# The 32 rows of u beside the gates: 8 matmuls of 512 columns and 8 of 256 in place of 24 of 256, and the sum of the two halves on ScalarE and VectorE

## The chip, the core and the metric

The kernel runs on one core of a Trainium2 chip. The metric is the device time of one execution in microseconds (us); the number of a kernel is the median over its runs.

## The reference

One launch computes two transformer blocks over 256 tokens of width 1024, in float32. The last part of the second block, an expert layer (PEER), is what the change touches. It has 128 x 128 experts; every token and each of 8 heads picks 16 of them, with a softmax weight (the gate) each.

```python
# x: (256, 1024) normed tokens; u, v: (16384, 1024), one row per expert
G[t, e] = sum over heads and picks of the softmax weight of token t for expert e
hid     = gelu_tanh(x @ u.T) * G          # (256, 16384)
h       = h + hid @ v
out     = rmsnorm(h) * final_norm_g_2
```

The kernel computes hid densely: 128 rows of u, each of 128 experts (128 x 1024 weights, 512 KB), and 128 rows of v of the same size.

## The kernel before

**Number format.** A product in full float32 precision is made of three products of rounded numbers (fp32r): w_hi * x_hi, w_hi * x_lo and w_lo * x_hi, all summed in PSUM. x_hi and x_lo stand beside each other in the tile `x_both`. ScalarE makes w_hi out of the raw weights (L426, two halves of 512 columns for a unit), another engine makes w_lo = raw - w_hi (L433). There are two buffers of w_hi and w_lo, so the split of a unit waits for the matmuls of the unit two before it, half by half (semaphores s_use1 for the first half, s_use for the second).

**Stages of the expert layer.** 36 rows of u are multiplied early, while the picks are made. Then comes the stage of the gates, in which this change lies: it makes the matrix G, 64 groups of 4 tokens, and multiplies 32 more rows of u beside it. In this text the rows of the stage are numbered r = 0 to 31, and groups A(r) = 2r and B(r) = 2r + 1 belong to row r. The gelu of each of these 68 rows goes to memory (`early_rows`) and comes back later. After this follow the stage of v (68 rows of v, L2985 before the change, `v_unit`), and a last stage with the remaining 60 rows of both.

**One row of the stage of the gates**, each engine in its own fixed order, written out by hand:
- VectorE (DVE), `hot_body`: for a group, one instruction that makes two one-hot matrices in bf16 (L2903, from an iota in SBUF and indices in PSUM), and three that multiply one of them by three pieces of the softmax weight (L2909). There are two buffers, so group n waits until the matmuls of group n - 2 are done (s_made).
- TensorE (PE), `made_body`: 12 bf16 matmuls of 128 columns for each group (L2920), when its one-hots are there (s_hot, s_gated). Then `u_products` for each half of the row: 8 matmuls with w_hi, 256 columns each, x_hi and x_lo in turn (L509), and 4 with w_lo (L515), all into the same 256 columns of `ps_chunk[r % 2]`.
- ScalarE (ACT): copies the two groups' 4 x 128 results out of PSUM (L2927, `kept_body`), splits w_hi for row r + 2 (L426, `ahead`), takes the gelu of row r straight from PSUM (L2811, `early_gelu`), and issues the DMA to `early_rows` (L2814).
- GpSimd (POOL): w_lo for row r + 2 (L433). SyncE (SP): loads of the raw units.

The last stage already has the layout that the change brings to this one: 512 columns in one matmul with w_hi (L3102), 256 with w_lo (L3110), a copy of the second half by ScalarE (L3160), the sum by VectorE (L3214), the gelu from SBUF (L3164).

Of the kernel before, what the change touches and what calls it, by code (L numbers as in the profile page):

```python
# [20 lines left out]
ALU = mybir.AluOpType  # L21
ACT = mybir.ActivationFunctionType
AX = mybir.AxisListType

P = 128
# [190 lines left out]
def build(nc, stream, cols, rows, consts0, consts1, consts2, x, mem, positions, small_w, cmp_w1, cmp_w2, peer_keys, p_t, out):  # L216
    ctx = ExitStack()
    with ctx:
# [2603 lines left out]
        def fetch(e, q, c=0):  # L2822

            i = c * 4 + q
            src = early[i, :, :] if isinstance(i, int) else early[bass.ds(i, 1), :, :].rearrange("a p n -> p (a n)")
            e.dma_start(gel[(q + 2) % 4], src).then_inc(s_back[q % 4], 16)
# [42 lines left out]
        def peer_gates():  # L2869
# [7 lines left out]
            s_hot, s_gated, s_made, s_kept = (sem(n) for n in ("s_hot", "s_gated", "s_made", "s_kept"))  # L2877
            groups = T // 4

            def loop(e, body):  # L2880

                for g in range(4):
                    body(e, g, g)
                with e.Fori(1, groups // 4) as i:
                    for g in range(4):
                        body(e, i * 4 + g, g)

            def after(e, s, n, back):

                if not isinstance(n, int) or n >= back:  # L2890
# [39 lines left out]
            def eight_rows(c, group, row):  # L2930
                for q in range(2 * UNITS):
                    for g in (2 * q, 2 * q + 1):
                        group(c * 16 + g, g % 4)
                    for part in range(2):
                        row(c, q, part)

            def tensor_gates(e):
                def row(c, q, part):
                    i = c * 8 + (EARLY_SELECT + q)
                    if part == 0:  # L2940
                        bank_left(e, i)
                    u_products(e, q % 2, q % 2, c * 8 + (u_early + EARLY_SELECT + q), range(4 * part, 4 * part + 4), part)
                group = lambda n, g: made_body(e, n, g)
                eight_rows(0, group, row)
                with e.Fori(1, EARLY_GATES // 8) as c:
                    eight_rows(c, group, row)

            def activation_gates(e):
                def row(c, q, part):
                    if part == 0:  # L2950
                        ahead(e, q % 4, c * 2 + (EARLY_SELECT // 4 + q // 4))
                    else:
                        early_gelu(e, q, c * 8 + (EARLY_SELECT + q))
                group = lambda n, g: kept_body(e, n, g)
                for i in range(2):
                    fetch(e, i)
                eight_rows(0, group, row)
                with e.Fori(1, EARLY_GATES // 8) as c:
                    eight_rows(c, group, row)

            dve.steps.append(lambda e: loop(e, hot_body))
            pe.steps.append(tensor_gates)
            act.steps.append(activation_gates)
            for lane in work:
# [459 lines left out]
```

## Time and profile before

| | |
|---|---|
| time, median of 3 runs | 1566.6 us (1566.23 to 1568.51) |
| the profiled execution: time / span | 1562.93 us / 1561.1 us |
| mean granted clock of TensorE | 0.989 of full speed |
| busy share of the span: PE, DVE, ACT, POOL | 97%, 76%, 56%, 23% |
| stage of the gates | from 898.4 us to about 1035.5 us of the span |

Read it so: the span is the time between the first and the last instruction of the profiled execution, and stage times are counted from its start. In the timeline a piece is a merged run of like instructions: its length reaches from the start of the first to the end of the last. Matmuls are pipelined, so that a matmul's own length is more than its distance to the next one; the chain of waits counts by those distances.

### The profile page before, as it was taken

How to read it: one execution, taken by the hardware profiler on the slowest of the kernel's cores; microseconds unless marked ns; L12 is line 12 of the kernel's file. 1: busy time of each engine (PE TensorE's matmuls, PEld its weight loads, DVE VectorE, ACT ScalarE, POOL GpSimd, SP SyncE). 2: the span in 40 equal slices, each digit the busy share in tenths (PEclk: the TensorE clock that was granted, in tenths of full speed). 3: DMA queues.
4: the chain of work that ended last, by engine and by line, in shares of the span. 5: the costliest groups of instructions: out<-in, count | busy, mean ns of one | idle time of the engine just before them, and what ended most of it. 6: DMA issues, size and time to landing. Idle time of an engine off the chain costs nothing.

```text
span 1561.1 us, 31498 instructions
## 1 busy us (share of the span) xinstructions
PE 1512.0 (97%) x10240; PEld 1349.4 (86%) x10240; DVE 1187.5 (76%) x2368; ACT 870.5 (56%) x1629; POOL 355.8 (23%) x265
## 2 busy tenths in 40 slices
PE   8899998999999899899999999999999999999997
PEld 8789987999887786698999999988888888888886
DVE  4788585789748578455489978889999777777777
ACT  5664444666548654566555566654444555555555
POOL 3334333011100331232068956630000000000000
PEclk9999999999999999999999999999999999999999
DMA  8333244555665720264557755467777666666665
GB/s 291 121 109 108 92 152 148 161 183 175 197 185 173 251 81 1 68 202 149 176 162 220 231 165 156 159 187 240 241 243 239 207 193 191 189 188 188 189 190 171
DMA packets 89289, 272.22 MB, mean 174 GB/s; under 512 B 9984, under 2 KB 27520, under 8 KB 88832
## 3 DMA queue, kind: packets, MB, share of 16 engines
q1 hardware_dynamic: 65520, 238.06, 48.7%
q10 hardware_dynamic: 23696, 33.17, 6.7%
q8 instruction: 48, 0.79, 0.2%
q14 instruction: 25, 0.20, 0.0%
HBM read 259.13 MB, written 12.06 MB: 174 GB/s over the span
## 4 chain that ended last, share of the span: by engine, by line
PE 88%; DVE 6%; ACT 3%; issue 1%; DMA 1%; POOL 0%; ACTq 0%; DVEq 0%; SPq 0%
PE ps_chunk L509 17%; PE ps_misc L2985 12%; PE ps_misc L502 10%; PE ps_chunk L502 9%; PE ps_chunk L515 8%; PE ps_chunk L3102 7%; PE ps_misc L301 7%; PE ps_chunk L1947 4%; PE ps_chunk L3110 4%; PE ps_misc L2920 3%; PE ps_chunk L301 3%; PE ps_chunk L521 1%; PE ps_chunk L530 1%; PE ps_misc L1025 1%; PE ps_chunk L525 1%
## 5 line engine op out<-in xcount | busy, mean ns | idle before, releaser
L426 ACT ACTIVATE w_hi<-raw 128x512 fp32r<-128x512 f32 (+2 forms) x654 | 399.8, 625 | 364.5 <-PE ps_chunk L515 142.7
L433 DVE TENSOR_TENSOR w_lo<-raw,w_hi 128x512 fp32r<-128x512 f32 (+1 forms) x419 | 317.4, 785 | 151.5 <-ACT w_hi L426 148.4
L433 POOL TENSOR_TENSOR w_lo<-raw,w_hi 128x512 fp32r<-128x512 f32 (+2 forms) x237 | 312.4, 1328 | 499.3 <-ACT w_hi L426 432.3
L509 PE MATMUL ps_chunk<-x_both,w_hi 128*128 128x256 f32 x2208 | 314.9, 285 | 0.8 <-ACT row L2811 0.5
L509 PEld LDWEIGHTS ps_chunk<-x_both,w_hi 128*128 128x128 f32 x2208 | 284.7, 192 | 1.3 <-issue 0.7
L515 PE MATMUL ps_chunk<-x_both,w_lo 128*128 128x256 f32 x1104 | 177.4, 283 | 0.0
L515 PEld LDWEIGHTS ps_chunk<-x_both,w_lo 128*128 128x128 f32 x1104 | 152.3, 192 | 0.1
L3200 DVE TENSOR_TENSOR w_lo<-raw,w_hi 128x512 fp32r<-128x512 f32 x120 | 83.0, 693 | 67.5 <-ACT w_hi L3154 67.4
L502 PE MATMUL ps_chunk<-w_hi,x_both 128*128 128x512 f32 (+1 forms) x392 | 123.4, 396 | 5.5 <-POOL w_lo L433 2.9
L3102 PE MATMUL ps_chunk<-x_both,w_hi 128*128 128x512 f32 x480 | 120.2, 392 | 0.0
L301 PE MATMUL ps_misc<-mixers_arena 128*128 128x128 f32 (+9 forms) x820 | 110.9, 303 | 7.9 <-ACT mixers_arena L1055 3.2
L301 PEld LDWEIGHTS ps_misc<-mixers_arena 128*128 128x128 f32 (+3 forms) x820 | 94.5, 188 | 22.0 <-issue 7.9
L3154 ACT ACTIVATE w_hi<-raw 128x512 fp32r<-128x512 f32 x120 | 75.7, 632 | 63.3 <-PE ps_misc L502 63.2
L2985 PE MATMUL ps_misc<-w_hi,hid_hi 128*128 128x512 f32 x272 | 105.9, 389 | 1.0 <-issue 1.0
L2985 PE MATMUL ps_misc<-w_hi,hid_lo 128*128 128x512 f32 x272 | 105.8, 389 | 0.0
L3102 PEld LDWEIGHTS ps_chunk<-x_both,w_hi 128*128 128x128 f32 x480 | 86.4, 189 | 15.5
L502 PE MATMUL ps_misc<-w_hi,hid_hi 128*128 128x512 f32 x236 | 91.8, 389 | 0.0
L502 PE MATMUL ps_misc<-w_hi,hid_lo 128*128 128x512 f32 x236 | 91.8, 389 | 0.0
L502 PE MATMUL ps_misc<-w_lo,hid_hi 128*128 128x512 f32 x236 | 91.8, 389 | 0.0
L3026 DVE TENSOR_TENSOR xn<-row,peer_arena 128x256 f32<-128x256 f32 x128 | 82.0, 640 | 10.2 <-PE ps_misc L2985 6.9
L502 PEld LDWEIGHTS ps_chunk<-w_hi,x_both 128*128 128x128 f32 x392 | 71.5, 192 | 20.6 <-POOL w_lo L433 3.9
L502 PE MATMUL ps_chunk<-x_both,w_hi 128*128 128x256 f32 x416 | 81.3, 291 | 5.2 <-DVE w_lo L433 3.0
(437 smaller groups left out, 2635.8 us busy)
## 6 DMA issues: line engine op xcount, KB each, us to landing
raw<-in_stream SPq DMA_DIRECT2D x452, 512.0 KB, 3.8
early_rows<-row ACTq DMA_DIRECT2D x68, 128.0 KB, 2.6
row<-early_rows ACTq DMA_DIRECT2D x66, 128.0 KB, 3.4
memory_kv<-mixers_arena ACTq DMA_DIRECT2D x4, 512.0 KB, 5.0
mixers_arena<-in_cmp_w ACTq DMA_DIRECT2D x1, 2048.0 KB, 9.3
mixers_arena<-memory_kv ACTq DMA_DIRECT2D x4, 512.0 KB, 6.4
mixers_arena<-in_consts ACTq DMA_DIRECT2D x1, 1729.0 KB, 8.3
row<-in_rows ACTq DMA_DIRECT2D x3, 512.0 KB, 6.7
```

What stands on the lines that cost most here:

```text
L301: return lambda e: e.matmul(out, lhsT, rhs, start=start, stop=stop, skip_group_check=True)
L426: e.activation(w_hi[q % 2][:, s], raw[q][:, s], ACT.Copy).then_inc(made, 1)
L433: e.tensor_tensor(w_lo[q % 2][:, s], raw[q][:, s], w_hi[q % 2][:, s].bitcast(F32), ALU.subtract).then_inc(made, 1)
L502: last = e.matmul(o, stationary[a], moving[b], start=start and i == 0, stop=stop and i == 2, skip_group_check=True)
L509: e.matmul(o, w[0][:, k * P:(k + 1) * P], x[:, k, :], start=k == 0 and x is x_hi, stop=False, skip_group_check=True)
L515: last = e.matmul(o, w[1][:, k * P:(k + 1) * P], x_hi[:, k, :], start=False, stop=k == KD - 1, skip_group_check=True)
L1947: return e.matmul(out(t, half), x[:, k, t * P:(t + 1) * P], w[u % 2][:, half * CW:(half + 1) * CW], start=start, stop=stop, skip_group_che ...
L2985: return e.matmul(ps_misc[:, 2 * t + half, :], x[:, b, t * P:(t + 1) * P], weights[w][:, half * CW:(half + 1) * CW], start=start, stop=Fal ...
L3026: e.tensor_tensor(own[b], gel[slot], g, ALU.mult).then_inc(s_own, 1)
L3102: last = e.matmul(ps_chunk[b][:, 0:2 * T], w_hi[0][:, k * P:(k + 1) * P], x_both[:, :, k, :], start=k == 0, stop=False, skip_group_check=True)
L3154: e.activation(w_hi[1][:, halves[half]], raw[q][:, halves[half]], ACT.Copy).then_inc(v_high[half], 1)
L3200: e.tensor_tensor(w_lo[1][:, halves[half]], raw[q][:, halves[half]], w_hi[1][:, halves[half]].bitcast(F32), ALU.subtract).then_inc(low_mad ...
```

## The change

It does four things in the stage of the gates.
1. TensorE: with w_hi, each of the 8 blocks of 128 rows takes one matmul of 512 columns (x_hi and x_lo together, into 512 columns of `ps_chunk`) in place of two of 256. Both halves of w_hi come first, then both halves of w_lo; the s_use1 signal of the first half is thus given later within the row than before.
2. ScalarE: it copies the second 256 columns out of PSUM to SBUF (`across`, which lies in gel[2:4]), then takes the gelu in place in SBUF, when VectorE has made the sum.
3. VectorE: the sum of the two halves, `two_halves(r)`, comes behind the one-hots of groups A(r+1) and B(r+1) and ahead of those of A(r+2) and B(r+2). The wait for the DMA that empties `gel` moves from ScalarE to this sum.
4. The two loads of early rows into gel[2] and gel[3] (`fetch`) move from ahead of the stage to behind it on ScalarE's queue.

```diff
             def tensor_gates(e):
                 def row(c, q, part):
                     i = c * 8 + (EARLY_SELECT + q)
+                    u = c * 8 + (u_early + EARLY_SELECT + q)
+                    b = q % 2
+                    tiles = [range(4 * half, 4 * half + 4) for half in range(2)]
                     if part == 0:
                         bank_left(e, i)
-                    u_products(e, q % 2, q % 2, c * 8 + (u_early + EARLY_SELECT + q), range(4 * part, 4 * part + 4), part)
+                        for half in range(2):
+                            e.wait_ge(high_of_half[half], u + 1)
+                            for k in tiles[half]:
+                                e.matmul(ps_chunk[b][:, 0:2 * T], w_hi[b][:, k * P:(k + 1) * P], x_both[:, :, k, :],
+                                         start=k == 0, stop=False, skip_group_check=True)
+                    else:
+                        for half, made, used_up in halves_of_unit:
+                            e.wait_ge(made, u + 1)
+                            low_weights(e, ps_chunk[b][:, 0:T], (None, w_lo[b]), tiles[half]).then_inc(used_up, 1)
...
             def activation_gates(e):
                 def row(c, q, part):
+                    i, b = c * 8 + (EARLY_SELECT + q), q % 2
                     if part == 0:
                         ahead(e, q % 4, c * 2 + (EARLY_SELECT // 4 + q // 4))
-                    else:
-                        early_gelu(e, q, c * 8 + (EARLY_SELECT + q))
+                        return
+                    e.wait_ge(s_use, i + (u_early + 1))
+                    if not isinstance(c, int) or q >= 2:
+                        e.wait_ge(s_two_sums, c * 8 + (q - 1))
+                    e.activation(across[b], ps_chunk[b][:, T:2 * T], ACT.Copy).then_inc(s_across, 1)
+                    e.wait_ge(s_two_sums, c * 8 + (q + 1))
+                    e.activation(gel[b], gel[b], ACT.Gelu_apprx_tanh).then_inc(s_gel, 1)
...
-                for i in range(2):
-                    fetch(e, i)
                 eight_rows(0, group, row)
                 with e.Fori(1, EARLY_GATES // 8) as c:
                     eight_rows(c, group, row)
-
-            dve.steps.append(lambda e: loop(e, hot_body))
+                for i in range(2):
+                    fetch(e, i)
+
+            def vector_gates(e):
+
+                def pair(r, q):
+                    for g in range(2):
+                        hot_body(e, r * 2 + g, 2 * q + g)
+
+                def two_halves(r, q):
+                    e.wait_ge(s_across, r + 1)
+                    e.wait_ge(s_spill[q], (r - q) * 8 + (EARLY_SELECT // 2 * 16))
+                    e.tensor_tensor(gel[q], ps_chunk[q][:, 0:T], across[q], ALU.add).then_inc(s_two_sums, 1)
+
+                pair(0, 0)
+                pair(1, 1)
+                two_halves(0, 0)
+                with e.Fori(1, EARLY_GATES // 2) as c:
+                    pair(c * 2, 0)
+                    two_halves(c * 2 - 1, 1)
+                    pair(c * 2 + 1, 1)
+                    two_halves(c * 2, 0)
+                two_halves(EARLY_GATES - 1, 1)
+
+            dve.steps.append(vector_gates)
```

How the instructions then stand in each engine's queue is shown at three places. The lines of the changed kernel are numbered anew: L2912 is L2920 of before (the groups' matmuls), L2919 is L2927 (the copies of the groups), L2895 and L2901 are L2903 and L2909 (the one-hots), L2943 is the new matmul of 512 columns.

**First place, one row in the queues of TensorE and ScalarE.** TensorE before, from the two groups of a row to the first group of the next:

```order
L2920 MATMUL ps_misc<-xn 128x128 x12
L2920 MATMUL ps_misc<-picks,xn 128x128 x12
L509 MATMUL ps_chunk<-x_both,w_hi 128x256 x8
L515 MATMUL ps_chunk<-x_both,w_lo 128x256 x4
L509 MATMUL ps_chunk<-x_both,w_hi 128x256 x8
L515 MATMUL ps_chunk<-x_both,w_lo 128x256 x4
```

And in the changed kernel:

```order
L2912 MATMUL ps_misc<-xn 128x128 x12
L2912 MATMUL ps_misc<-picks,xn 128x128 x12
L2943 MATMUL ps_chunk<-x_both,w_hi 128x512 x8
L515 MATMUL ps_chunk<-x_both,w_lo 128x256 x8
L2912 MATMUL ps_misc<-xn 128x128 x12
```

The 16 matmuls with w_hi became 8, and the first 4 with w_lo moved behind all those with w_hi.

ScalarE in the changed kernel, one row and the start of the next (`row` is the tile in which `gel` and `across` lie; L2963 is the copy across, L2965 the gelu):

```order
L2919 ACTIVATE peer_arena<-ps_misc 128x512 x2
L426 ACTIVATE w_hi<-raw 128x512 x2
L2963 ACTIVATE row<-ps_chunk 128x256
L2965 ACTIVATE row<-row 128x256
L2968 DMA early_rows<-row 128x256
L2919 ACTIVATE peer_arena<-ps_misc 128x512 x2
```

Before, one gelu out of `ps_chunk` (L2811) stood where the copy and the gelu stand now; the copy across stands behind both splits of w_hi.

**Second place, VectorE from the one-hots of row 1 to those of row 2** in the changed kernel (L2985 is now `two_halves`; the three rows behind it begin the loop):

```order
L2895 TENSOR_TENSOR xn<-xn,ps_chunk 128x1024
L2901 TENSOR_TENSOR xn<-xn,ps_misc 128x4x128 x3
L2895 TENSOR_TENSOR xn<-xn,ps_chunk 128x1024
L2901 TENSOR_TENSOR picks<-xn,ps_misc 128x4x128 x3
L2985 TENSOR_TENSOR row<-ps_chunk,row 128x256
L2990 UNCONDITIONAL_BRANCH
L2990 ISA
L2895 ISA
L2895 TENSOR_TENSOR xn<-xn,ps_chunk 128x1024
```

Before, the one-hots followed one another with nothing between them; now the sum of row 0 stands behind the one-hots of row 1 and ahead of those of row 2.

**Third place, VectorE where the stage of the gates ends and that of v begins** (L3062, L3064 and L3066 are the gate, the rounding and the remainder of `gate_row`, L3026, L3028 and L3030 before):

```order
L2984 ISA
L2985 TENSOR_TENSOR row<-ps_chunk,row 128x256
L2990 REGISTER_ALU
L2990 COMPARE_AND_BRANCH
L2985 TENSOR_TENSOR row<-ps_chunk,row 128x256
L3062 TENSOR_TENSOR xn<-row,peer_arena 128x256
L3064 CAST hid_hi<-xn 128x256
L3066 TENSOR_TENSOR hid_lo<-xn,hid_hi 128x256
```

The sum of row 31 stands ahead of the first `gate_row`, which had followed the last one-hots directly.

## Rows read from the trace of the kernel before

**Rows 1.** The page, busy time, share of the span and instructions of each engine.

```profile
PE 1512.0 (97%) x10240; PEld 1349.4 (86%) x10240; DVE 1187.5 (76%) x2368; ACT 870.5 (56%) x1629; POOL 355.8 (23%) x265
```

**Rows 2.** Windows: busy time of each engine in two stretches, PEclk, DMA share, GB/s.

```profile
580.00:590.00 10.00, 9.31 (x73) 6.17 (x74) 8.84 (x27) 3.97 (x13) 0.00 (x0) 0.78 0.00 0
...
930.00:962.00 32.00, 32.00 (x356) 31.70 (x355) 25.87 (x61) 19.93 (x38) 18.51 (x15) 1.00 0.52 151
```

**Rows 3.** The chain that ended last, gates stage: start us, length us, what.

```profile
924.23 1.36 PE ps_misc L2920 x24
925.59 1.01 PE ps_chunk L509 x8
926.60 0.48 PE ps_chunk L515 x4
927.08 0.96 PE ps_chunk L509 x8
...
928.51 0.52 PE ps_misc L2920 x9
```

**Rows 4.** The same chain in the last stage.

```profile
1354.15 1.84 PE ps_chunk L3102 x8
...
1358.71 0.95 PE ps_chunk L3110 x8
```

**Rows 5.** Timeline, one row of the gates: start, length, engine, line [idle before <-releaser].

```profile
927.87 0.64 PE L515 MATMUL ps_chunk<-x_both,w_lo 128*128 128x256 f32 x4
...
928.55 0.63 ACT L426 ACTIVATE w_hi<-raw 128x512 fp32r<-128x512 f32 x1 [0.74 <-PE ps_chunk L515]
929.03 0.83 PE L2920 MATMUL ps_misc<-picks,xn 128*128 128x128 bf16 x12
929.09 0.36 ACT L2811 ACTIVATE row<-ps_chunk 128x256 f32<-128x256 f32 x1
929.37 0.69 DVE L2903 TENSOR_TENSOR xn<-xn,ps_chunk 128x1024 bf16<-128x1024 bf16 x1 [0.49 <-PE ps_misc L2920]
...
929.87 1.09 ACT L2927 ACTIVATE peer_arena<-ps_misc 128x512 f32<-128x512 f32 x2 [0.41 <-PE ps_misc L2920]
...
932.08 1.08 DVE L2909 TENSOR_TENSOR picks<-xn,ps_misc 128x512 bf16<-128x512 bf16 x3 [0.17 <-DVE xn L2903]
932.15 0.64 PE L515 MATMUL ps_chunk<-x_both,w_lo 128*128 128x256 f32 x4
```

**Rows 6.** Timeline, the same hand-offs in the last stage.

```profile
1303.42 1.11 PE L3110 MATMUL ps_chunk<-x_both,w_lo 128*128 128x256 f32 x8
...
1304.65 0.39 ACT L3160 ACTIVATE xn<-ps_chunk 128x256 f32<-128x256 f32 x1 [0.40 <-PE ps_chunk L3110]
...
1305.49 0.42 DVE L3214 TENSOR_TENSOR row<-ps_chunk,xn 128x256 f32<-128x256 f32 x1
1305.83 0.68 DVE L3194 TENSOR_TENSOR w_lo<-raw,w_hi 128x512 fp32r<-128x512 f32 x1
1305.95 0.42 ACT L3164 ACTIVATE row<-row 128x256 f32<-128x256 f32 x1 [0.91 <-DVE row L3214]
```

**Rows 7.** Timeline, where the gates stage ends and the stage of v begins.

```profile
1034.00 0.64 DVE L3026 TENSOR_TENSOR xn<-row,peer_arena 128x256 f32<-128x256 f32 x1 [2.40 <-ACT peer_arena L2927]
...
1034.87 0.64 PE L515 MATMUL ps_chunk<-x_both,w_lo 128*128 128x256 f32 x4
1034.88 2.70 POOL L433 TENSOR_TENSOR w_lo<-raw,w_hi 128x512 fp32r<-128x512 f32 x2 [1.62 <-ACT w_hi L426]
1035.00 1.44 DVE L3030 TENSOR_TENSOR hid_lo<-xn,hid_hi 128x256 fp32r<-128x256 f32 x1
...
1036.48 1.59 DVE L3026 TENSOR_TENSOR xn<-row,peer_arena 128x256 f32<-128x256 f32 x1
...
1036.54 0.47 PE L2985 MATMUL ps_misc<-w_hi,hid_hi 128*128 128x512 f32 x1 [1.03 <-issue]
...
1038.43 0.42 DVE L3030 TENSOR_TENSOR hid_lo<-xn,hid_hi 128x256 fp32r<-128x256 f32 x1
```

More of the change, by code:

```diff
@@ L2878, in peer_gates @@
             groups = T // 4
[L2880 to L2886, printed above, removed]
             def after(e, s, n, back):
@@ L2935, in eight_rows @@
                         row(c, q, part)
+            s_across, s_two_sums = sem("s_across"), sem("s_two_sums")
+            across = gel[2:4]
             def tensor_gates(e):
@@ L2949, in row @@
                 def row(c, q, part):
+                    i, b = c * 8 + (EARLY_SELECT + q), q % 2
                     if part == 0:
                         ahead(e, q % 4, c * 2 + (EARLY_SELECT // 4 + q // 4))
-                    else:
-                        early_gelu(e, q, c * 8 + (EARLY_SELECT + q))
+                        return
[5 more added lines that the diff above has]
+                    e.activation(gel[b], gel[b], ACT.Gelu_apprx_tanh).then_inc(s_gel, 1)
+                    e.wait_ge(s_gel, i + 1)
+                    dst = early[i, :, :] if isinstance(i, int) else early[bass.ds(i, 1), :, :].rearrange("a p n -> p (a n)")
+                    e.dma_start(dst, gel[b]).then_inc(s_spill[b], 16)
                 group = lambda n, g: kept_body(e, n, g)
-                for i in range(2):
-                    fetch(e, i)
                 eight_rows(0, group, row)
```

## The prediction

> **What bounds the kernel now.** I read the page first: TensorE is busy 97% of the span [rows 1], so time can only be won where TensorE gets less to do, and is lost wherever it is made to wait. Then the windows: in the stage of the gates TensorE is busy 32.00 of 32 us at a granted clock of 1.00, VectorE 25.87, ScalarE 19.93, GpSimd 18.51 [rows 2]. Then the chain that ended last, which gives TensorE's true pace: one row of the stage takes 928.51 - 924.23 = 4.28 us. Of these the two groups take 1.36, the first 8 matmuls with w_hi 1.01 (0.05 more than the second 8, 0.96, on the change from bf16), and each four with w_lo 0.48 [rows 3]. So a matmul of 256 columns takes a step of 0.12. The last stage shows what a matmul of 512 columns costs there: 8 take 1.84, a step of 0.23, and 8 of 256 take 0.95 [rows 4].
>
> Then the timeline of one row, for what surrounds TensorE [rows 5]. I call E(r) the end of the last matmul with w_lo of row r as the timeline gives it (932.15 + 0.64 = 932.79), and B(r) the start of the row's second group (929.03). Before the change nobody behind TensorE is late for it: VectorE waits 0.49 for TensorE's groups and then needs 932.08 + 1.08 - 929.37 = 3.79 for the one-hots of the next row; ScalarE is idle until TensorE releases it.
>
> **The change part by part.**
>
> *TensorE.* With w_hi, 16 steps of 0.12 (1.92) become 8 of 0.23 (1.84). The w_lo matmuls and the groups stay. That is 0.08 a row, so a row bound by TensorE would take 4.20, and 32 rows give back 2.6 us. It is small because two matmuls of 256 columns already run nearly at the price of one of 512. The bounds of the gain are nothing (0.24 against 0.24) and 0.12 a row (0.01 of rounding either way in the step, times 8, and no entry cost of 0.05); I take 0.08.
>
> *The added wait.* VectorE's queue now holds: one-hots of row r+1, sum(r), one-hots of row r+2. The sum needs the copy across of row r, and this needs the end of row r on TensorE. Behind the waiting sum stand the one-hots of row r+2, for which TensorE's group B(r+2) waits. So a ring closes over two rows: E(r), copy, sum, one-hots of r+2, B(r+2), E(r+2). Its links:
> 1. E to copy. The copy stands behind both splits of w_hi. The first split waits for the first four w_lo matmuls, which now end only 0.48 ahead of E (before, they ended a whole half row earlier). With 0.10 for the hand-off (between 0.04, from 928.51 to 928.55 [rows 5], and 0.12, from 1304.53 to 1304.65 [rows 6]) it starts at E - 0.38. From one split to the next instruction on ScalarE it takes 0.54 (928.55 to 929.09 [rows 5]), so the second split starts at E + 0.16, the copy at E + 0.70.
> 2. The copy takes 0.39, to E + 1.09, and the hand-off to VectorE 0.04 (that from VectorE to ScalarE, 1305.91 to 1305.95, is the nearest [rows 6]): the sum starts at E + 1.13.
> 3. From the start of the sum to the next VectorE instruction 0.34 (1305.49 to 1305.83 [rows 6]): E + 1.47.
> 4. The one-hots of a row, 3.79 [rows 5]: E + 5.26.
> 5. Hand-off to TensorE 0.10 (1035.00 + 1.44 = 1036.44 to 1036.54 [rows 7]): B(r+2) = E(r) + 5.36.
> 6. B to E was 3.76 (929.03 to 932.79 [rows 5]), less the 0.08 won: 3.68.
>
> The ring is 9.04 us for two rows, 4.52 a row, against 4.28 before and 4.20 of TensorE alone. VectorE's own work is no bound: at most 3.79 + 0.34 = 4.13. ScalarE's is not either, but it is near. The sum ends at E + 1.55; the gelu takes 0.42 [rows 6], to E + 2.01; from the end of the gelu to the copies of the groups 0.42 passed (929.45 to 929.87, with the DMA issue in it [rows 5]), and these take 1.09, to E + 3.52, while the next first split is due at E + 4.20 - 0.38 at the earliest. GpSimd's w_lo and the loads have more than a row of room.
>
> Rows 0 and 1 have their one-hots before any sum, so B(1) comes 4.20 after B(0); then 15 rings lead from B(1) to B(31). In all 4.20 + 15 x 9.04 = 139.8, where before 31 x 4.28 = 132.7 passed: +7.1. The last row is 0.08 shorter: **+7.0 us** for the stage. Within a ring the two rows need not be equal: 4.20 and 4.84 in turn is as good.
>
> *The end of the stage.* TensorE's first matmul with v came 1.03 after E (1034.87 + 0.64 = 1035.51 to 1036.54 [rows 7]), since the first gate row was made while row 31 still ran. Now sum(31) stands ahead of it: it starts at E + 1.13, gate row 0 at E + 1.47. Its three instructions take 1.42 when nothing disturbs them (1034.00 to 1035.00, and 0.42 for the last), which would put v at E + 2.99, 2.0 later than before. But the remainder took 1.44 at 1035.00 where it takes 0.42 at 1038.43, and the next gate 1.59 where the one before took 0.64; both lie within GpSimd's 2.70 us of splitting, and end at or soon after the end of one of its instructions [rows 7]. GpSimd's split for the second unit of v will lie at about E + 0.3 to E + 3.0 (the first split ends at E - 0.38 + 0.63, and it works 2.70), so the first gate row falls into it: the remainder then ends some 0.25 after that and v starts at E + 3.4. I take **+2.4**; the bounds are 1.9, and 3.9 with both waits as long as in those rows (1.02 and 0.95). The Trainium skill, SBUF — State Buffer, section Who interferes with whom, states that a VectorE instruction with two SBUF inputs is blocked by a GpSimd one that reads SBUF; the trace agrees (1.44 for 0.42).
>
> *The fetches.* Moved behind the stage, they are issued near E + 2.5 to 3.4; the third gate row, their first reader, is due only when the first v unit has been used: 12 steps of 0.23 after E + 3.4, at E + 6.2. That leaves them about 3 us to land; no row shown here has the landing, and what it takes beyond 3 us would come on top. I put it at nothing. Nothing later gives the time back: TensorE is at its own pace in the stages that follow.
>
> The sum: 7.0 + 2.4 = +9.4 us. The profiled execution had 1562.93 us with a span of 1561.1, so it would become 1572.3; on the median of 1566.6, which is 3.7 above it, this is **1576 us** (+0.6%).
>
> **How far the ring may be off.** The low end takes 0.04 for each hand-off and 0.34 for the copy: some 0.2 a ring, -3 us, with the tail at 1.9: 1572.5. The high end adds 0.3 a ring for waits whose register values are computed between the instructions, and a ScalarE that comes late by the longer gap ahead of its copies: +4.5, with the tail at 3.9: 1582.
>
> **The rivals.**
> - *The ring does not bind* (chance 0.11). If VectorE's one-hots needed about half a microsecond less, or the copy came before the splits, TensorE would keep its 4.20: -2.6 for the stage, +2.0 to 2.4 for its end: 1566 us, no change that can be told. Against it stands 3.79 in rows 5, which is steady. From 8.40 down the ring no longer decides.
> - *Faster* (0.03): as above, and the end of the stage costs nothing too: 1563 us or a little less. Only the 0.08 a row speaks for it; rows 4 allow no more.
> - *The sum collides with GpSimd* (0.06). GpSimd splits w_lo from about E + 0.3 to E + 3.0, just when the sum runs. If the sum behaved as the remainder did (1.44 for 0.42), the ring would be 10.06 and VectorE's own work 5.1 a row: 15 x 1.02 = 15 us more, 1591. The sum has one input in PSUM, and the one-hots, which also have one, run at a steady 3.79 beside GpSimd [rows 5]: against it. By the skill's page named above, an instruction with one SBUF input does not contend.
> - *The clock falls* (0.04). TensorE now idles some 0.3 us a row. At a granted clock of 0.78, as in one stretch of broken work with 9.31 of 10 us busy [rows 2], a row would take 4.20 / 0.78 = 5.4, and the stage 35 us more: about 1603. Against it: the idle here is shorter and the work between denser; other stretches with more idle kept 1.00. The Trainium skill, TensorE: Matmul & The Clock Gate, section A second HAM failure mode: psum-queue depth-cycling, describes such falls from frequent short idle; no row of this stage shows one.
>
> **How the numbers follow.** The forecast (1572 to 1583) has 0.76. About 3.1 us, 0.2%, is what can be told from no change here. Slower: 0.76 + 0.06 + 0.04 = 0.86. Same: 0.11. Faster: 0.03. To leave out no more than 2 in 10, and to take in the bounds of links and tail, the range is 1570 to 1586.
>
> **What would show it right or wrong.** In the changed profile, groups B (L2912 with `picks`) should wait for VectorE's L2901, in total 7 to 10 us; L2985 should follow L2963 within 0.1 with VectorE idle before it (about 0.4 a row); the gelu L2965 should wait for L2985; the stage should take some 144 us where it took 137, with row lengths of 4.2 and 4.8 in turn or 4.5 each; 8 matmuls L2943 should take 1.84; L2985 0.42; v should start 3 to 4 us after the last w_lo matmul. If no wait of TensorE for VectorE is seen, the ring is wrong; if L2985 takes over a microsecond, GpSimd is the cause; a PEclk below 1.00 in the stage speaks for the clock.

## The result, and the profile after

The change makes the kernel slower: a median of 1583.97 us (6 runs, 1578.6 to 1590.75) against 1566.41 us before, ratio 1.0102, 95% interval 1.0084 to 1.0119. By the ratio that is 16 us (the two medians are 17.6 us apart); the forecast was 1576, with a range of 1570 to 1586.

First the page of the changed kernel, busy time of each engine, which answers to [rows 1], and then windows (columns as in [rows 2]): one in the middle of the stage, and one at the start of the stage of v.

```profile
PE 1516.1 (96%) x9984; PEld 1337.6 (85%) x9984; DVE 1198.7 (76%) x2400; ACT 880.5 (56%) x1661; POOL 353.9 (22%) x265
```
```profile
930.00:962.00 32.00, 28.79 (x275) 25.56 (x274) 26.21 (x64) 19.63 (x41) 17.63 (x14) 1.00 0.47 140
```
```profile
1056.00:1061.00 5.00, 4.78 (x14) 3.82 (x15) 1.78 (x5) 1.04 (x2) 0.00 (x0) 0.66 0.91 280
```

TensorE has less to do and still takes longer: it is idle for 3.2 of 32 us in a stretch where it was never idle [rows 2]. Its granted clock stayed at 1.00 there, but in the second window, behind the stage, it was 0.66.

Who waits for whom between 895 and 1060 us (engine, line, waited for: total us, times, longest):

```profile
ACT row L2965 <- DVE row L2985: 20.8, 32, 0.8
...
DVE row L2985 <- ACT row L2963: 17.5, 17, 3.7
...
PE ps_misc L2912 <- DVE picks L2901: 9.2, 12, 0.8
...
PE ps_misc L3021 <- issue: 3.9, 1, 3.9
```

The forecast chain is all there: the sum (L2985) waits for the copy across (L2963), and TensorE's groups B wait for the one-hots (L2901). The timeline of two rows shows the order in time; it answers to [rows 5]:

```profile
925.31 1.11 PE L515 MATMUL ps_chunk<-x_both,w_lo 128*128 128x256 f32 x8
...
926.04 1.15 ACT L426 ACTIVATE w_hi<-raw 128x512 fp32r<-128x512 f32 x2 [1.01 <-PE ps_chunk L515]
...
926.94 0.83 PE L2912 MATMUL ps_misc<-picks,xn 128*128 128x128 bf16 x12
927.10 0.36 ACT L2963 ACTIVATE row<-ps_chunk 128x256 f32<-128x256 f32 x1
...
927.60 0.42 DVE L2985 TENSOR_TENSOR row<-ps_chunk,row 128x256 f32<-128x256 f32 x1 [0.82 <-ACT row L2963]
...
928.28 0.69 DVE L2895 TENSOR_TENSOR xn<-xn,ps_chunk 128x1024 bf16<-128x1024 bf16 x1 [0.26 <-issue]
...
930.99 1.08 DVE L2901 TENSOR_TENSOR picks<-xn,ps_misc 128x512 bf16<-128x512 bf16 x3 [0.17 <-DVE xn L2895]
...
931.99 0.42 DVE L2985 TENSOR_TENSOR row<-ps_chunk,row 128x256 f32<-128x256 f32 x1
932.18 0.83 PE L2912 MATMUL ps_misc<-picks,xn 128*128 128x128 bf16 x12 [0.87 <-issue]
932.33 0.68 DVE L2895 TENSOR_TENSOR xn<-xn,ps_chunk 128x1024 bf16<-128x1024 bf16 x1
...
936.39 0.83 PE L2912 MATMUL ps_misc<-picks,xn 128*128 128x128 bf16 x12
```

E is 925.31 + 1.11 = 926.42. The splits start at E - 0.38, the copy at E + 0.68, the sum at E + 1.18, the next one-hots at E + 1.86; they end at 932.07 and group B starts 0.11 later (the profile books that wait under "issue", but it ends with them). The groups B start at 926.94, 932.18 and 936.39: 5.24 and 4.21 apart, the unequal rows of a ring of two. Over the stage, B(0) is at 904.1 and B(31) at 1048.65 (timeline), so a ring takes (144.5 - 4.2) / 15 = 9.35 us on average. The ring shown is one of the first and a little longer: from E = 926.42 to 934.76 + 1.11 = 935.87 it takes 9.45. In the rings from E = 945.27 on, the copy that the waiting sum needs starts at E + 0.62, not + 0.68, and the groups B are 4.22 and 5.13 apart.

**Where the time went.** First and last start of two groups of matmuls of the changed kernel, then of the kernel before in a second profile of it, `before_again` (lines L2912 and L3021 are L2920 and L2985 of before; after the start times stands the form):

```profile
L2912 PE MATMUL ps_misc<-xn x384: 219/219/230, 903.4 to 1048.6; 128*128 128x128 bf16 x192
...
L3021 PE MATMUL ps_misc<-w_hi,hid_hi x272: 387/389/628, 1056.2 to 1242.0; 128*128 128x512 f32 x136
```
```profile
L2920 PE MATMUL ps_misc<-xn x384: 219/219/230, 901.4 to 1034.7; 128*128 128x128 bf16 x192
...
L2985 PE MATMUL ps_misc<-w_hi,hid_hi x272: 389/389/470, 1039.5 to 1223.7; 128*128 128x512 f32 x136
```

From the first of A(0) to the first with v ("the stage length" below) it is 152.8 us after and 138.1 before: +14.7. The stage of v takes 185.8 in place of 184.2: +1.6. From the last matmul with v to the end of the span it is 340.4 us in the first profiles of both. That makes 16.3 us, where the ratio says 16. The two first profiled executions differ by 21.3 us; the 5.0 that remain lie ahead of the stage, which began at 898.4 and 903.4.

### The profile page after: what moved, and what is told of

Its sections match the earlier page's. It is cut to its first block, busy times and chain, and to the rows that moved or that the text cites. A ratio compares the mean times of both kernels' runs of the same rounds, so it can differ in the third digit from the quotient of the medians.

```text
span 1582.4 us, 31120 instructions
## 1 busy us (share of the span) xinstructions
PE 1516.1 (96%) x9984; PEld 1337.6 (85%) x9984; DVE 1198.7 (76%) x2400; ACT 880.5 (56%) x1661; POOL 353.9 (22%) x265
## 4 chain that ended last, share of the span: by engine, by line
PE 83%; DVE 8%; ACT 4%; issue 3%; DMA 1%; DVEq 1%; POOL 0%; ACTq 0%; SPq 0%
PE ps_chunk L509 13%; PE ps_misc L3021 12%; PE ps_misc L502 10%; PE ps_chunk L502 10%; PE ps_chunk L515 7%; PE ps_chunk L3138 7%; PE ps_misc L301 6%; PE ps_chunk L1947 4%; PE ps_chunk L3146 4%; PE ps_chunk L2943 2%; PE ps_chunk L301 2%; PE ps_chunk L521 1%; PE ps_misc L2912 1%; ACT w_hi L426 1%; DVE xn L2895 1%
## 5 line engine op out<-in xcount | busy, mean ns | idle before, releaser
L433 DVE TENSOR_TENSOR w_lo<-raw,w_hi 128x512 fp32r<-128x512 f32 (+1 forms) x419 | 320.8, 793 | 155.1 <-ACT w_hi L426 152.0
L509 PE MATMUL ps_chunk<-x_both,w_hi 128*128 128x256 f32 x1696 | 241.8, 285 | 0.9 <-ACT row L2811 0.5
L509 PEld LDWEIGHTS ps_chunk<-x_both,w_hi 128*128 128x128 f32 x1696 | 220.4, 193 | 1.5 <-issue 0.7
L515 PE MATMUL ps_chunk<-x_both,w_lo 128*128 128x256 f32 x1104 | 172.2, 283 | 0.0
L3021 PE MATMUL ps_misc<-w_hi,hid_hi 128*128 128x512 f32 x272 | 106.6, 392 | 3.9 <-issue 3.9
L3021 PE MATMUL ps_misc<-w_hi,hid_lo 128*128 128x512 f32 x272 | 106.4, 391 | 0.0
L3138 PEld LDWEIGHTS ps_chunk<-x_both,w_hi 128*128 128x128 f32 x480 | 86.4, 189 | 15.5
L3062 DVE TENSOR_TENSOR xn<-row,peer_arena 128x256 f32<-128x256 f32 x128 | 80.9, 632 | 10.4 <-PE ps_misc L3021 9.6
L502 PE MATMUL ps_chunk<-x_both,w_hi 128*128 128x256 f32 x416 | 81.9, 292 | 4.7 <-DVE w_lo L433 3.0
```

The costliest lines, as they stand in the source:

```text
L433: e.tensor_tensor(w_lo[q % 2][:, s], raw[q][:, s], w_hi[q % 2][:, s].bitcast(F32), ALU.subtract).then_inc(made, 1)
L502: last = e.matmul(o, stationary[a], moving[b], start=start and i == 0, stop=stop and i == 2, skip_group_check=True)
L509: e.matmul(o, w[0][:, k * P:(k + 1) * P], x[:, k, :], start=k == 0 and x is x_hi, stop=False, skip_group_check=True)
L515: last = e.matmul(o, w[1][:, k * P:(k + 1) * P], x_hi[:, k, :], start=False, stop=k == KD - 1, skip_group_check=True)
L3021: return e.matmul(ps_misc[:, 2 * t + half, :], x[:, b, t * P:(t + 1) * P], weights[w][:, half * CW:(half + 1) * CW], start=start, stop=Fal ...
L3062: e.tensor_tensor(own[b], gel[slot], g, ALU.mult).then_inc(s_own, 1)
```

## The experiments

Except where said, each is an edit of the changed kernel. The stage length is read as above.

| kernel | stage length us | ratio to before, 95% interval |
|---|---|---|
| before, before_again | 138.1, 138.1 | 1.0002 (0.9984 to 1.002) |
| changed, changed_again | 152.8, 152.8 | 1.0102 (1.0084 to 1.0119), 1.0101 (1.0065 to 1.0136) |
| copy_first | 144.7 | 1.0043 (1.0029 to 1.0058) |
| narrow | 153.9 | 1.0101 (1.0081 to 1.0121) |
| half_by_half | 151.6 | 1.0123 (1.0103 to 1.0144) |
| loop_turned | 148.0 | 1.0083 (1.0067 to 1.0099) |
| unrolled | 142.6 | 1.0036 (1.0019 to 1.0054) |
| last_sum_later | 150.9 | 1.0108 (1.0092 to 1.0125) |
| sum_between | 167.0 | 1.0185 (1.0165 to 1.0205) |
| kept_ahead | 143.8 | 1.0052 (1.0033 to 1.0072) |
| all_moved | 139.9 | 1.0017 (1.0001 to 1.0034) |
| all_unrolled | 134.8 | 0.9981 (0.9966 to 0.9996) |

**Is it the ring? copy_first.**

```diff
                     if part == 0:
+                        e.wait_ge(s_use, i + (u_early + 1))
+                        if not isinstance(c, int) or q >= 2:
+                            e.wait_ge(s_two_sums, c * 8 + (q - 1))
+                        e.activation(across[b], ps_chunk[b][:, T:2 * T], ACT.Copy).then_inc(s_across, 1)
                         ahead(e, q % 4, c * 2 + (EARLY_SELECT // 4 + q // 4))
                         return
-                    e.wait_ge(s_use, i + (u_early + 1))
-                    if not isinstance(c, int) or q >= 2:
-                        e.wait_ge(s_two_sums, c * 8 + (q - 1))
-                    e.activation(across[b], ps_chunk[b][:, T:2 * T], ACT.Copy).then_inc(s_across, 1)
```

> ScalarE copies the second half of row r out of PSUM ahead of its two splits of w_hi, not behind them; nothing else differs from the changed kernel. In this and the later expectations the stage length is the time from the first matmul of group A(0) to the first matmul with v: 138.1 us before, 152.8 us in the changed kernel. Ring theory (end of row r, copy, sum, one-hots of r+2, group B(r+2), row r+2 closes over two rows at 9.35 us): the copy moves from 0.68 us to about 0.08 us behind the end of the row, the ring becomes 8.75, 15 rings give back 9 us: stage length 143 to 144, time some 7 us above before (ratio about 1.005). Rival, the lost time is in VectorE's port shared with GpSimd or in the order of the matmuls: no change to the changed kernel, ratio 1.010.

The stage takes 1046.4 - 901.7 = 144.7 us and the ratio is 1.0043: nearly what the ring theory had (143 to 144, 1.005), and far from the rival's "no change". Moving one copy by 0.6 us gave back 8 us over the stage; no work changed.

**Is it the matmuls? narrow and half_by_half.** As written, narrow leaves out a part of its sums (probably the product of the first block with x_hi; no run shows which); number and size of its instructions are as said.

```diff
-                                e.matmul(ps_chunk[b][:, 0:2 * T], w_hi[b][:, k * P:(k + 1) * P], x_both[:, :, k, :],
-                                         start=k == 0, stop=False, skip_group_check=True)
+                                for s in range(2):
+                                    e.matmul(ps_chunk[b][:, s * T:(s + 1) * T], w_hi[b][:, k * P:(k + 1) * P],
+                                             x_both[:, s, k, :], start=k == 0, stop=False, skip_group_check=True)
```

> The changed kernel with its queues as they are, but each matmul of 512 columns is done as two of 256 again (x_hi into the first half, x_lo into the second): 24 matmuls of 256 columns a row as before the change. It separates the width of the matmuls from the new dependences. Ring theory: 0.08 us more a row, so 1.2 to 2.5 us above the changed kernel, ratio to before 1.011 to 1.012. Rival, the matmuls of 512 columns themselves are what costs: the time falls back towards before.

The stage is 1.1 us longer than in the changed kernel (1062.5 - 908.6 = 153.9), as 15 rings of 0.08 more would make it; the time can't be told from the changed kernel's. The width of the matmuls is worth about a microsecond, and the loss is not in it.

half_by_half:

```diff
-                        for half in range(2):
+                        for half, made, used_up in halves_of_unit:
                             e.wait_ge(high_of_half[half], u + 1)
...
-                    else:
-                        for half, made, used_up in halves_of_unit:
                             e.wait_ge(made, u + 1)
                             low_weights(e, ps_chunk[b][:, 0:T], (None, w_lo[b]), tiles[half]).then_inc(used_up, 1)
```

> Only the order of the matmuls within a row of the changed kernel goes back: w_hi and w_lo of the first half, then of the second, with 512 columns for w_hi. The split of the first half of w_hi can then start 1.4 us ahead of the end of the row and not 0.4 us. Ring theory: the second split still waits for the end of the row, so the copy across comes only some 0.1 us earlier (0.6 in place of 0.7 behind the end), 15 rings of 9.25: the stage is 1 to 2 us shorter than 152.8, the ratio 1.009. Rival, the reordering of the w_lo matmuls (the late release of w_hi) is the cause of the loss: the time falls back to about before.

The stage got 1.2 us shorter (1055.9 - 904.3 = 151.6), the size the ring gives. The time shows no gain (1.0123 where 1.009 was expected, with an interval that overlaps the changed kernel's), but the rival, a return to about before, is out.

**The term that was too small: loop_turned and unrolled.** From the start of a sum to the next one-hots I had 0.34; behind a sum that has waited it is 0.68 (927.60 to 928.28), behind one that has not, 0.34 (931.99 to 932.33). The changed kernel's chain of waits at such a place (start us, length us, what; DVEq is VectorE's own control instructions):

```profile
937.05 0.07 DVE row L2985
...
937.14 0.06 DVEq L2990
937.20 0.26 issue
937.46 0.07 DVEq L2990
...
937.73 0.70 DVE xn L2895
```

L2990 is the line of the loop. The sum that waits is the last of the loop's body, so the branch is taken only when the wait has ended.

```diff
                 pair(0, 0)
                 pair(1, 1)
-                two_halves(0, 0)
                 with e.Fori(1, EARLY_GATES // 2) as c:
+                    two_halves(c * 2 - 2, 0)
                     pair(c * 2, 0)
                     two_halves(c * 2 - 1, 1)
                     pair(c * 2 + 1, 1)
-                    two_halves(c * 2, 0)
+                two_halves(EARLY_GATES - 2, 0)
                 two_halves(EARLY_GATES - 1, 1)
```

> The changed kernel with VectorE's loop begun at another point of the same order: its body is sum(2c-2), one-hots of row 2c, sum(2c-1), one-hots of row 2c+1, so that the loop's branch no longer stands behind a sum that waits, but behind one-hots. No work and no order changes. In the changed kernel the chain shows 0.34 us of loop instructions and issue between the start of the waiting sum and the next one-hots, beyond the 0.34 us that follow a sum that has not waited. Theory: they are the branch, and the ring falls from 9.35 by about 0.3 to about 9.05: stage 147 to 149 us where the changed kernel has 152.8, ratio about 1.007. Rival, any instruction behind a wait restarts that late: nothing changes.

In its timeline the one-hots follow a sum that waited after 0.35:

```profile
934.28 0.42 DVE L2985 TENSOR_TENSOR row<-ps_chunk,row 128x256 f32<-128x256 f32 x1 [0.68 <-ACT row L2963]
...
934.63 0.68 DVE L2895 TENSOR_TENSOR xn<-xn,ps_chunk 128x1024 bf16<-128x1024 bf16 x1
```

The stage takes 148.0 us and the ratio is 1.0083: the branch was 4.8 us of the stage. With it out, the ring is (139.7 - 4.2) / 15 = 9.03. That this is the forecast's 9.04 is partly luck, as the section on the prediction shows.

unrolled writes all 32 rows out (`for r in range(1, EARLY_GATES): pair(r, r % 2); two_halves(r - 1, (r - 1) % 2)`):

> VectorE's loop over the rows of the stage is written out (32 rows), so that no register instruction stands between the sum and the next one-hots; the order is that of the changed kernel. There the next instruction started 0.68 us after the start of a sum that had waited, and 0.34 us after one that had not. Theory: the 0.34 is register work that VectorE's sequencer can only do after the wait; without it the ring falls from 9.35 to about 9.0 and the stage from 152.8 to 147 to 148 us, ratio about 1.007. Rival: it is the restart after a wait as such, and nothing changes.

It gained more than expected: 142.6 where 147 to 148 was expected. A ring is (134.4 - 4.2) / 15 = 8.68, which is 0.67 less than in the changed kernel. The branch accounts for 0.34. The sum now starts 0.04 behind the end of the copy in place of 0.14 (957.15 + 0.36 = 957.51 to 957.55). And the one-hots of a row (from L2895 to the end of the last L2901) now take 3.51 in place of 3.79, for within a group the step from L2895 to L2901 is 0.71 (962.04 to 962.75) in place of 0.86 (928.28 to 929.14). The copy itself varies by 0.06 from ring to ring, so these three (0.34 + 0.10 + 0.28 = 0.72) need not add up exactly.

```profile
961.70 0.42 DVE L2985 TENSOR_TENSOR row<-ps_chunk,row 128x256 f32<-128x256 f32 x1 [0.30 <-ACT row L2963]
962.04 0.68 DVE L2895 TENSOR_TENSOR xn<-xn,ps_chunk 128x1024 bf16<-128x1024 bf16 x1
...
962.75 1.08 DVE L2901 TENSOR_TENSOR xn<-xn,ps_misc 128x512 bf16<-128x512 bf16 x3
...
964.47 1.08 DVE L2901 TENSOR_TENSOR picks<-xn,ps_misc 128x512 bf16<-128x512 bf16 x3
```

**The end of the stage: last_sum_later.** In the changed kernel it looks so (timeline):

```profile
1051.22 1.11 PE L515 MATMUL ps_chunk<-x_both,w_lo 128*128 128x256 f32 x8
...
1053.41 0.42 DVE L2985 TENSOR_TENSOR row<-ps_chunk,row 128x256 f32<-128x256 f32 x1 [3.74 <-ACT row L2963]
1053.75 0.63 DVE L3062 TENSOR_TENSOR xn<-row,peer_arena 128x256 f32<-128x256 f32 x1
...
1054.42 1.25 DVE L3064 CAST hid_hi<-xn 128x256 fp32r<-128x256 f32 x1
...
1055.70 0.42 DVE L3066 TENSOR_TENSOR hid_lo<-xn,hid_hi 128x256 fp32r<-128x256 f32 x1
...
1056.22 0.47 PE L3021 MATMUL ps_misc<-w_hi,hid_hi 128*128 128x512 f32 x1 [3.90 <-issue]
...
1058.22 0.63 PE L3021 MATMUL ps_misc<-w_hi,hid_lo 128*128 128x512 f32 x1
1058.65 0.63 PE L3021 MATMUL ps_misc<-w_hi,hid_hi 128*128 128x512 f32 x1
```

TensorE waits 3.90 us for the first gate row. Behind that its matmuls of 512 columns come at a step of 0.23 for the first 1.2 us, then, until about 1060.8, at 0.43 (1058.22 to 1058.65): of the clock's two levels, 1.2 GHz in place of 2.4. Before, with 1.03 us idle [rows 7], the granted clock was 1.00 from 1036 to 1041 us. The edit calls the last sum in `vector_early`, behind the first `gate_row`:

```diff
                             gate_row(e, q, q, q, EARLY - 2 + q)
+                            if q == 0:
+                                last_sum[0]()
                             continue
```

> Only the sum of row 31 moves: it comes behind the first gate row of the stage of v. Tail theory: TensorE's idle time ahead of v falls from 3.9 us to about 1, and with it goes the stretch at the lower clock that followed (matmuls of 512 columns at a step of 0.43 us for 3.4 us): together 4.5 us less than the changed kernel, ratio to before about 1.007. If the low clock has another cause, only 2.9 us less. Rival, the first gate row is late for another reason (the fetches moved behind the stage): no change.

This missed (4.5 us less in all and a ratio of 1.007 expected). The stage is only 1.9 us shorter, and the time can't be told from the changed kernel's. Its timeline shows why:

```profile
1049.94 1.09 ACT L2921 ACTIVATE peer_arena<-ps_misc 128x512 f32 x2 [0.72 <-ACT row L2967]
...
1051.06 0.62 DVE L3064 TENSOR_TENSOR xn<-row,peer_arena 128x256 f32<-128x256 f32 x1 [2.29 <-ACT peer_arena L2921]
...
1053.51 0.77 PE L3023 MATMUL ps_misc<-w_hi,hid_hi 128*128 128x512 f32 x1 [2.08 <-issue]
...
1059.86 0.63 DVE L3064 TENSOR_TENSOR xn<-row,peer_arena 128x256 f32<-128x256 f32 x1 [4.05 <-DMA row<-early_rows]
...
1061.41 0.49 PE L3023 MATMUL ps_misc<-w_hi,hid_hi 128*128 128x512 f32 x1 [0.62 <-DVE hid_lo L3068]
```

The first gate row now waits for ScalarE's copies of groups A(31) and B(31), which stand behind the gelu of row 30; TensorE is idle 2.08 us, and the clock falls all the same (matmuls of 0.63 again). And the third gate row waits for the fetch, which I had put at nothing: VectorE is idle 4.05 us for it, and TensorE 0.62.

**Can the ring be opened? sum_between, kept_ahead, all_moved, all_unrolled.** The sum is put between the one-hots of the two groups:

```diff
+                    for q in range(2):
+                        hot_body(e, c * 4 + 2 * q, 0)
+                        two_halves(c * 2 + (q - 2), q)
+                        hot_body(e, c * 4 + (2 * q + 1), 1)
...
```

> VectorE makes the sum of row r between the one-hots of group A(r+2) and those of group B(r+2), not ahead of both. Ring theory: only one group's one-hots (1.9 us) stand behind the waiting sum, the ring falls to about 7.5 us for two rows and no longer decides; TensorE runs at its own 4.20 a row, the stage is 14 us shorter than in the changed kernel (138 to 139 us) with the late first gate row left in, and the time is 1 to 4 us above before (ratio 1.001 to 1.003). Rival, VectorE has too much work (its sum stalls on GpSimd or its issue takes longer): the row stays at 4.6 us whatever the order.

It missed by far: 167.0 us where 138 to 139 was expected, the slowest kernel of all, with a row of 5.2 us in the place shown. Its timeline:

```profile
942.46 0.83 PE L2912 MATMUL ps_misc<-xn 128*128 128x128 bf16 x12 [0.80 <-DVE picks L2901]
...
943.46 0.69 DVE L2895 TENSOR_TENSOR xn<-xn,ps_chunk 128x1024 bf16<-128x1024 bf16 x1 [1.02 <-PE ps_misc L2912]
...
944.32 1.09 DVE L2901 TENSOR_TENSOR xn<-xn,ps_misc 128x512 bf16<-128x512 bf16 x3 [0.17 <-DVE xn L2895]
945.32 0.42 DVE L2985 TENSOR_TENSOR row<-ps_chunk,row 128x256 f32<-128x256 f32 x1
...
945.77 0.42 ACT L2965 ACTIVATE row<-row 128x256 f32<-128x256 f32 x1 [1.66 <-DVE row L2985]
...
946.94 1.08 ACT L2919 ACTIVATE peer_arena<-ps_misc 128x512 f32 x2 [0.74 <-ACT row L2965]
...
947.68 0.83 PE L2912 MATMUL ps_misc<-xn 128*128 128x128 bf16 x12 [0.87 <-DVE picks L2901]
```

Group A at 942.46, one-hots of the next A, sum, gelu, copy of group A, next group A at 947.68: a ring of one row, 5.22 us. It closes because ScalarE copies the groups of row r+1 behind the gelu of row r. The profile names VectorE as releaser of the last row; its one-hots for this group had been done since 944.32 + 1.09 = 945.41, so by the order of the queues it is the copy (the first of the two copies at 946.94 ends near 947.5). The next experiment tests that.

kept_ahead puts, on ScalarE, the two copies of row r+1 between the copy across and the gelu of row r:

```diff
+                        row(c, q, 0)
+                        for g in (2 * q + 2, 2 * q + 3):
+                            if not (last and g > 15):
+                                kept_body(e, c * 16 + g, g % 4)
...
+                        row(c, q, 1)
```

> The sum stands between the one-hots of groups A(r+2) and B(r+2), as in sum_between, and ScalarE copies the groups of row r+1 ahead of the gelu of row r, not behind it. In sum_between a second ring had closed over one row at 5.22 us: group A on TensorE, one-hots of the next A, sum, gelu, copy of group A, next A. With the copies ahead of the gelu that ring is open as well. Two-rings theory: TensorE's own pace of 4.20 a row remains, the stage falls from 167 us in sum_between (152.8 in the changed kernel, 138.1 before) to 136 to 140 us, time within 0 to 4 us of before (ratio 1.000 to 1.003). Rival, the sum between the one-hots is itself what slows VectorE: the row stays near 5.2 us.

The second ring is open: 143.8 us, 23 less than sum_between. But this missed too (136 to 140, ratio 1.000 to 1.003 expected; 1.0052 measured): the row is (1033.9 - 898.4) / 31 = 4.37, not TensorE's 4.20, and the pause of 3.90 us ahead of v is still there. all_moved adds the last sum behind the first gate row, as in last_sum_later, and the fetch into gel[2] ahead of the last gelu:

```diff
+                        if last and q == 7 and True:
+                            e.wait_ge(s_two_sums, EARLY_GATES - 1)
+                            fetch(e, 0)
                         row(c, q, 1)
```

> kept_ahead, and also the end of the stage mended: the sum of row 31 comes behind the first gate row, and the fetch into gel[2] is issued ahead of the last gelu. If the row is at 4.20 us, the first matmul with v comes within 2 us of the end of row 31, and the clock does not fall ahead of v, since TensorE is not idle in the stage: stage length 134.5 to 137 us, time 0 to 3 us below before (ratio 0.998 to 1.000). Rival, the fall of the clock at the start of v has nothing to do with idle time in the stage: 2 us more.

139.9 us and 1.0017, where 134.5 to 137 and 0.998 to 1.000 were expected. TensorE went into v without a pause, and no matmul of v shows the lower clock (the longest of 512 columns lasted 0.50 us, in the changed kernel 0.63), but the stage of v was as long as in the changed kernel, 185.7 us: the second gate row came late (last line below). And the stage of the gates is not at TensorE's pace throughout. Two groups B in its timeline, and the matmul of v that waited:

```profile
1029.89 0.84 PE L2914 MATMUL ps_misc<-picks,xn 128*128 128x128 bf16 x12
...
1034.41 0.84 PE L2914 MATMUL ps_misc<-picks,xn 128*128 128x128 bf16 x12
...
1046.49 0.50 PE L3036 MATMUL ps_misc<-w_hi,hid_hi 128*128 128x512 f32 x1 [1.16 <-DVE hid_lo L3081]
```

The groups are 4.52 apart, and it is 4.22 to the next. all_unrolled is all_moved with VectorE's rows written out:

```diff
+                for r in range(EARLY_GATES - 2):
+                    hot_body(e, 2 * r + 4, 0)
+                    two_halves(r, r % 2)
+                    hot_body(e, 2 * r + 5, 1)
```

> all_moved with VectorE's rows written out as in unrolled. In all_moved a row still took 4.39 us on average: the chain group A(r+1) on TensorE, its successor's one-hots, the sum, the one-hots of group B(r+2), group B(r+2) takes 5.2 us where TensorE's own pace leaves 4.88. Written out, the one-hots of a group take some 0.17 us less, the chain 4.8, and TensorE should run at 4.20 a row: stage 133.5 to 136 us where all_moved had 139.9 and before 138.1; time 1 to 3 us below before (ratio 0.998 to 0.9995). Rival, something else holds the row at 4.3 to 4.4 us: ratio as all_moved, 1.0017.

The chain of waits is TensorE alone, with a row of 953.01 - 948.81 = 4.20:

```profile
948.81 1.36 PE ps_misc L2914 x24
950.16 1.90 PE ps_chunk L2945 x8
...
953.01 1.36 PE ps_misc L2914 x24
```

The stage takes 1037.2 - 902.4 = 134.8 us, 3.3 less than before, and the ratio is 0.9981 (0.9966 to 0.9996): the layout of the change does pay its 0.08 us a row, once no engine waits in the wrong place. Writing out VectorE's rows could not have won this alone: before, TensorE was never idle in the middle of the stage [rows 2]. But not all of the 3.3 us is the layout: the pause ahead of v fell from 1.03 us to 0.02. And the stage of v keeps 1.4 us of loss (185.6 for 184.2), for the second gate row is as late as in all_moved (TensorE waits 1.15 us for it).

**Is the code ahead of the stage delayed? before_again and changed_again.**

> The kernel before, profiled once more. It tells how much the stages ahead of the gates vary from one execution to the next: group A(0) began at 898.4 us in the profile of before and between 897.7 and 908.6 in those of nine other kernels, whose code ahead of it is the same. Expected: the stage of the gates again at 138.1 us within 0.3, its start anywhere from 897 to 906 us. If the change itself had delayed the stages ahead of it, the start would be at 898.4 again.

> The changed kernel, profiled once more. Expected: the stage again at 152.8 us within 0.3, rows of 4.20 and 5.14 us in turn, and the low clock behind the idle time ahead of v; the start of the stage anywhere from 897 to 906 us, no later on average than that of before_again.

Stage lengths repeat to the tenth (138.1 and 152.8). The starts are at 901.4 and 902.4, so the 5.0 us by which the first profile of the changed kernel was late at A(0) belong to that execution.

## Why the prediction was right, and where its sizes were off

**The mechanism was right.** The sum's wait on VectorE, with the one-hots of row r+2 behind it, closes a ring over two rows. It is shown, not argued: making one link shorter on ScalarE (copy_first) or on VectorE (loop_turned, unrolled) shortens the stage by about 15 times what it takes off the ring, with TensorE's work unchanged; and with the waits of all_unrolled TensorE is back at 4.20 us a row. The forecast of unequal rows held (4.22 and 5.13 in most rings, for 4.20 and 4.84).

**The links.** Forecast against the timeline above: copy at E + 0.70, measured 0.68, and 0.62 in most rings; copy 0.39, measured 0.36; one-hots 3.79, measured 3.79; hand-off to TensorE 0.10, measured 0.11; B to E 3.68, measured 3.69 (926.94 to 929.52 + 1.11). The hand-off to the sum was 0.14, not 0.04. The forecast had taken it from a hand-off the other way, VectorE to ScalarE. Inside the loop a control instruction of VectorE (L2984, 0.05) stands on the path there; outside the loop the hand-off is 0.04 (the last sum: 1053.01 + 0.36 = 1053.37 to 1053.41), as in unrolled. The forecast's high end had named such waits, its middle had not priced them. The mis-sized term is link 3, "from the start of the sum to the next VectorE instruction": 0.68, not 0.34. The row it came from [rows 6] is of a sum whose next instruction stood ready; here the loop's branch stood behind a wait. loop_turned measured it: 4.8 us of the stage. The other links nearly cancel: + 0.10 for the hand-off, - 0.08 and - 0.03 for the start and length of the copy. So without the branch the ring is the forecast's, though not every link is: that is luck. The whole ring is 9.35 for 9.04, and from B(0) to B(31) 144.5 passed for 139.8.

**The gain.** 0.08 us a row was right: in all_unrolled the row is 4.20. Two side figures do not follow from their terms: the gain's upper bound of 0.12 a row (0.08 + 0.08 + 0.05 is 0.21), and the 1563 us of "faster" (1566.6 - 2.6 = 1564.0). Nothing else rests on them.

**The end of the stage.** Forecast: v at E + 3.4, 2.4 later than before. Measured: E + 3.89, 2.9 later. That it collides with GpSimd was right in kind, but another instruction was hit: the rounding took 1.25 where it takes 0.29, and the remainder, which the forecast had slowed, took its 0.42 behind it. The clock had been a rival for the stage, where it stayed at 1.00 though TensorE was idle for a tenth of the time; it fell behind the idle time at the end, which the forecast had not priced: +1.6 us in the stage of v, which is what some eight steps of 0.43 in place of 0.23 come to. all_moved, where TensorE does not pause there, does not show the fall.

**The sum.** 9.4 was forecast and 16.3 measured: 4.7 more in the ring, 0.5 in the wait for v, 1.6 in the clock, which makes 6.8 of the 6.9. The high end (1582) had room for slower links, not for the clock. The measured 1583.97 lies above this high end, and inside the range only by the margin that the range has beyond it: the mechanism and the direction were foreseen, the size was not, and that the range holds it is in part luck.

**The signs.** Most came as named: the gelu waits for the sum, L2985 takes 0.42, v starts 3.89 us behind E. Groups B waited 11.5 us in all (9.2 for L2901 and 2.3 booked under "issue") where 7 to 10 was named.

**The rivals.** The sum did not collide with GpSimd: L2985 took 0.42 (415 to 426 ns in 32 cases), with one input in PSUM. The Trainium skill, SBUF — State Buffer, section Who interferes with whom, says that a VectorE instruction with at most one SBUF input does not contend, outside the modes in which it uses two ports; for the sum the trace agrees. The condition matters, and the prediction left it out: the rounding (L3064) also has one SBUF input, and it took 1.25 beside GpSimd's split in place of 0.29. "The ring does not bind" and "faster" are out. The fetches were not free once the gate rows came early (TensorE waited 0.62 us for the third one in last_sum_later).

## What to carry to other kernels

A wait put into an in-order queue costs what stands behind it: follow the ring of queues round, over as many rows as there are buffers, before counting the saving; here 0.08 us a row was bought with a wait that cost 0.5 a row. Where an instruction must wait, let nothing stand directly behind it that another engine needs soon, nor a loop's branch. Opening one ring can close another (sum_between), so check every queue on which the moved instruction is waited for.

## What the runs showed of the hardware

- A loop's branch on VectorE behind an instruction that waits costs 0.34 us on the path: 0.68 against 0.34 from a sum to the next instruction, 0.35 with the branch moved behind the one-hots. The way into the loop does not show it: behind the sum of row 0, which had waited 1.04, the next instruction started after 0.36.
- Written-out rows take 0.15 us less from L2895 to L2901 than rows in a loop (0.71 for 0.86), though both wait for the same semaphore of the engine itself. In the loop the chain of waits has a control instruction of VectorE (0.09) between the two, written out it has none. That this is the computing of the awaited value in a register is likely, and not tested.
- Two matmuls of 256 columns (0.24) cost nearly what one of 512 does (0.23 to 0.24; 8 took 1.90 in this stage, with the entry from bf16).
- The clock fell to the lower level about the start of v in all ten profiles in which TensorE had paused 2.08 to 4.19 us there, and in none of the four in which it had paused 1.03 us or less. Within the rows it stayed at 1.00 with 0.9 us of idle every 9.4, and in sum_between even with 4.7 us idle of 30 (935 to 965 us). What decides it stays open.
